# Hybrid decoder step: one dense group of the last mLSTM chunk placed behind the sums of the latent squares

## The reference

```python
def layer(x, ...):
    h = rmsnorm(x, lw['norm_mix'])
    z = h @ lw['w_in']
    qm, km, vm, om, im, fm, cq, ckv, kr = jnp.split(z, splits, axis=-1)
    hm, C, n, m = mlstm_chunkwise(qm, km, vm, ig, lf, C0, n0, m0)
    hm = rmsnorm(hm, lw['m_norm']) * jax.nn.sigmoid(om)
    lat = concatenate([rmsnorm(ckv, lw['mla_kv_norm']), rope(kr, pos)])
    qa = rmsnorm(cq, lw['mla_q_norm']) @ lw['mla_w_uq']
    ...   # latent attention, output projection, ConvFFN, embedding gate
```

## Time and profile before

| | us |
|---|---|
| median of three runs | 3328.66 |
| lowest, highest | 3320.07, 3329.58 |
| profiled execution | 3329.29 |
| its span | 3327.5 |
| mean granted clock, share of full | 0.958 |

### The profile page before, as it was taken

The page is one execution under the profiler, slowest core; times in us unless marked ns, Lnnn a source line. Parts: engine busy times, 40 slices in busy tenths (PEclk is TensorE's granted clock), DMA queues, the critical chain, the costliest instruction groups (busy, mean ns, idle before and its releaser), DMA issues. The chain is left out here.

```text
span 3327.5 us, 49163 instructions
## 1 busy us (share of the span) xinstructions
PE 3087.8 (93%) x19219; PEld 2874.2 (86%) x19219; DVE 1524.3 (46%) x2458; ACT 1067.3 (32%) x1982; POOL 144.3 (4%) x260
## 2 busy tenths in 40 slices
PE   4999999889999999988989999989899999999887
PEld 4998755789999999988989986559899999999886
DVE  4223643345454554447351345434554544454653
ACT  4323332324333323334242342322432323233341
POOL 0000300000000000000000012000000000000000
PEclk9999999889999999998989988989899999999988
DMA  5101252211111111102131023421111111111023
GB/s 212 52 26 44 86 172 70 103 56 51 39 39 52 46 44 51 39 18 90 40 123 41 16 99 101 133 60 81 68 40 50 51 39 51 39 39 51 6 103 131
DMA packets 60916, 220.53 MB, mean 66 GB/s; under 512 B 6922, under 2 KB 26890, under 8 KB 45842
## 3 DMA queue, kind: packets, MB, share of 16 engines
q1 hardware_dynamic: 60690, 217.27, 18.5%
HBM read 189.72 MB, written 27.52 MB: 65 GB/s over the span
## 5 line engine op out<-in xcount | busy, mean ns | idle before, releaser
L210 PE MATMUL psum<-h_high,conv_ffn_weight_parts 128*128 128x352 f32 x2112 | 690.4, 327 | 21.9 <-DVE h_low L315 14.3
L212 PE MATMUL psum<-h_high,conv_ffn_weight_parts 128*128 128x352 f32 x2112 | 686.7, 325 | 0.0
L211 PE MATMUL psum<-h_low,conv_ffn_weight_parts 128*128 128x352 f32 x2112 | 682.6, 323 | 0.0
L1990 DVE SCALAR_TENSOR_TENSOR conv_sum<-u_padded,vectors,conv_sum 128x1024 f32<-128x1024 f32 x176 | 226.1, 1285 | 595.1 <-ACT conv_sum L1939 582.6
L210 PEld LDWEIGHTS psum<-h_high,conv_ffn_weight_parts 128*128 128x128 f32 x2112 | 400.8, 190 | 24.9 <-issue 22.0
L211 PEld LDWEIGHTS psum<-h_low,conv_ffn_weight_parts 128*128 128x128 f32 x2112 | 399.3, 189 | 0.0
L212 PEld LDWEIGHTS psum<-h_high,conv_ffn_weight_parts 128*128 128x128 f32 x2112 | 397.1, 188 | 0.0
L210 PE MATMUL psum<-g_parts,conv_ffn_weight_parts 128*128 128x352 f32 x1056 | 345.3, 327 | 27.1 <-DVE g_parts L2001 16.3
L212 PE MATMUL psum<-g_parts,conv_ffn_weight_parts 128*128 128x352 f32 x1056 | 343.1, 325 | 0.0
L211 PE MATMUL psum<-g_parts,conv_ffn_weight_parts 128*128 128x352 f32 x1056 | 342.8, 325 | 0.0
L2009 DVE TENSOR_TENSOR x<-x,psum 128x352 f32<-128x352 f32 x528 | 255.5, 517 | 118.3 <-PE psum L212 117.9
(11 more groups left out here) (330 smaller groups left out, 5389.5 us busy)
## 6 DMA issues: line engine op xcount, KB each, us to landing
conv_ffn_weight_stage<-w_up_dram SPq DMA_DIRECT2D x44, 1024.0 KB, 4.8
conv_ffn_weight_stage<-w_down_dram SPq DMA_DIRECT2D x22, 1024.0 KB, 4.8
_projection_weight_stage<-w_in_dram SPq DMA_DIRECT2D x18, 1024.0 KB, 4.8
pages<-cache_dram SPq DMA_DIRECT2D x64, 288.0 KB, 4.2
pages<-cache_dram SPq DMA_DIRECT2D x64, 160.0 KB, 2.5
mix_work<-x_residual SPq DMA_DIRECT2D x16, 528.0 KB, 3.8
x<-x_residual SPq DMA_DIRECT2D x2, 4224.0 KB, 17.0
x_residual<-x SPq DMA_DIRECT2D x16, 528.0 KB, 2.7
```

The source lines that it names most:

```text
L210: pe.matmul(out, lhs[0], rhs[0], start=first, stop=False)
L211: pe.matmul(out, lhs[0], rhs[1], start=False, stop=False)
L212: return pe.matmul(out, lhs[1], rhs[0], start=False, stop=last)
L1990: dve.scalar_tensor_tensor(t[:, q, 0:SEQ], row[:, tap:tap + SEQ], w, t[:, q, 0:SEQ], ALU.mult, ALU.add).then_inc(ph["conv_step"], 1)
```

## The change

In the last chunk (c = 7) TensorE starts with `spread(7)` and no dense group in front of it. The first two dense groups then stand where the second and the third stood, and the third is issued after the sums of the latent squares; after it come the wait for the last evacuation and the transposes. The sums go to banks `B_S` and `B_S + 1` (5 and 6) instead of 0 and 1. ScalarE in the last chunk does `decays(7)` before it evacuates the first group, and after the second evacuation takes the square roots, `squares(7)`, and the last evacuation. VectorE takes the reciprocal between the outputs and the state updates of chunk 7 instead of at its end. SyncE's program is as it was.

```diff
--- before.py
+++ after.py
@@ -669,6 +669,9 @@
                     dve.tensor_tensor(vTM[:, c, i::2, 0:M_DV], num[:, i, :, 0:M_DV],
                                       den[:, 1, i::2].unsqueeze(2).to_broadcast([P, 2, M_DV]),
                                       ALU.mult).then_inc(ph["h_made"], 1)
+                if c == NCK - 1:
+                    dve.wait_ge(ph["rt_step"], 2)
+                    dve.reciprocal(mem.rt[:, 1], mem.rt[:, 0]).then_inc(ph["rs_made"], 1)
                 dve.wait_ge(ph["qa_made"], 3 * (c + 1))
                 for h in range(M_HEADS):
                     s = state[part(h), h // 2, :]
@@ -712,8 +715,6 @@
                 outputs(c)
                 if c in (1, 3):
                     ring.lo(dve, 7 + c // 2, JW)
-            dve.wait_ge(ph["rt_step"], 2)
-            dve.reciprocal(mem.rt[:, 1], mem.rt[:, 0]).then_inc(ph["rs_made"], 1)
 
         @block.scalar
         def _(act):
@@ -818,18 +819,23 @@
             act.wait_ge(ph["state_zeroed"], 2)
             act.wait_ge(ph["cwc_made"], 2)
             for c in range(NCK):
-                evacuate(MIXED + 3 * c)
+                if c < NCK - 1:
+                    evacuate(MIXED + 3 * c)
                 decays(c)
                 if 4 <= c < 7:
                     latent_squares(c)
+                if c == NCK - 1:
+                    evacuate(MIXED + 3 * c)
                 evacuate(MIXED + 3 * c + 1)
-                evacuate(MIXED + 3 * c + 2)
-                if c == NCK - 1:
-                    for i, d in enumerate((Q_RANK, KV_RANK)):
-                        act.wait_ge(ph["lsum_done"], i + 1)
-                        act.activation(mem.rt[:, 0, i, :], ps[:, i, 0:TT], ACT.Sqrt, bias=core.eps,
-                                       scale=1.0 / d).then_inc(ph["rt_step"], 1)
-                squares(c)
+                if c < NCK - 1:
+                    evacuate(MIXED + 3 * c + 2)
+                    squares(c)
+            for i, d in enumerate((Q_RANK, KV_RANK)):
+                act.wait_ge(ph["lsum_done"], i + 1)
+                act.activation(mem.rt[:, 0, i, :], ps[:, B_S + i, 0:TT], ACT.Sqrt, bias=core.eps,
+                               scale=1.0 / d).then_inc(ph["rt_step"], 1)
+            squares(NCK - 1)
+            evacuate(len(GROUPS) - 1)
 
         @block.tensor
         def _(pe):
@@ -919,20 +925,29 @@
             pe.wait_ge(ph["ones_made"], 1)
             pe.wait_ge(ph["state_zeroed"], 3)
             pe.wait_ge(ph["cwc_made"], 2)
-            for c in range(NCK):
+            def latent_sums(i, squares):
+                for c in range(TT):
+                    mm = pe.matmul(ps[:, B_S + i, c:c + 1], squares[:, token_tile(c)], core.ones[:, 0:1],
+                                   start=(c == 0), stop=True, skip_group_check=True)
+                mm.then_inc(ph["lsum_done"], 1)
+
+            for c in range(NCK - 1):
                 dense(MIXED + 3 * c)
                 spread(c)
                 dense(MIXED + 3 * c + 1)
                 scores(c)
                 dense(MIXED + 3 * c + 2)
                 values(c)
+            spread(NCK - 1)
+            dense(len(GROUPS) - 3)
+            scores(NCK - 1)
+            dense(len(GROUPS) - 2)
+            values(NCK - 1)
+            pe.wait_ge(ph["lsq_added"], 3)
+            latent_sums(0, core.norm)
+            latent_sums(1, mem.sqk)
+            dense(len(GROUPS) - 1)
             pe.wait_ge(ph["bank_free"], len(GROUPS))
-            pe.wait_ge(ph["lsq_added"], 3)
-            for i, squares in enumerate((core.norm, mem.sqk)):
-                for c in range(TT):
-                    mm = pe.matmul(ps[:, i, c:c + 1], squares[:, token_tile(c)], core.ones[:, 0:1],
-                                   start=(c == 0), stop=True, skip_group_check=True)
-                mm.then_inc(ph["lsum_done"], 1)
             pe.wait_ge(ph["rs_made"], 1)
             for c in range(TT):
                 tr = pe.transpose(ps[:, c // 4, c % 4 * P:(c % 4 + 1) * P],
```

## The result

| | before | changed |
|---|---|---|
| median, us | 3325.55 (6 runs, 3320.07 to 3329.58) | 3336.82 (6 runs, 3331.30 to 3339.20) |
| ratio | | 1.0033, 95% interval 1.0019 to 1.0047 |
| span of the profiled run, us | 3327.5 | 3330.0 |

The change costs 11.3 us by the medians, between 6 and 16 by the interval. The forecast stood on the median of the three runs taken first, 3328.66; all six runs of before have 3325.55, and against that median the forecast of +11.6 us reads 3337.2, where 3336.8 was measured. Of the 3.5 us between the recorded 3340.3 and the measured time, 3.1 are this shift of the base.

What follows compares the result with a forecast made beforehand. The prediction took whichever engine is last at the `mix_projection` barrier to set the price, with TensorE busy 93% of the span. Its terms summed to +5.8 us per layer, +11.6 over two, giving 3340.3 us from 3328.66; range 3331 to 3349.

Steps and rivals of the forecast that it cites:

- stall in front of `spread(7)`: Chunk 7: without a dense group as cover, TensorE idles until chunk 6's outputs are made; +1.0 us per layer.
- clock at `spread` and the group behind: Chunk 7: after the idle time the clock falls late in `spread`, slowing the dense group behind; +2.0 us per layer.
- latent sums: After `values(7)`: the sums still lose the clock but take 5.7 us; -0.6 us per layer, from -2.3 to +0.7.
- held-back group at low clock: Behind the sums: the third dense group begins at the low clock they left; +1.7 us per layer, 0 to +3.2.
- evacuation, transposes, stores: Phase end: the state store, delayed by the last evacuation, lands last at the barrier; +1.7 us per layer, +1.4 to +2.3.
- Rival A: Chunk 7: the clock is not lost at `spread(7)`, only in the sums; 3.8 us per layer, 3336.3 us, chance 0.18.
- Rival B: Last chunk: the clock is kept altogether because dense work follows at once; +0.4 us per layer, 3329.5 us, chance 0.08.
- Rival C: Phase end: the state store is hidden, tail 0 to 0.1 us; 4.1 us per layer, 3336.9 us, chance 0.1.
- Rival D: Phase end: held-back group wholly at half clock and store late; 7.9 us per layer, 3344.5 us, chance 0.12.
- Rival E: Last chunk: the group is not held back in effect because another wait binds; 3328.7 us, chance 0.02.

Runs made afterwards that it cites:

- wide sums: The changed kernel with each matmul of the latent sums streaming 128 columns of ones instead of one; 1.0016 of the kernel before.
- state store first: The changed kernel with the mLSTM state store put ahead of the last out-gate store in SyncE's order; 1.0032 of the kernel before.
- early half: The changed kernel with the third dense group moved back in front of the sums and the end ordered as before; 1.0024 of the kernel before.
- its two variants with wide sums: The kernel before with 128-column latent sums alone, 0.9996 of before; and with the sums of squares opening seven phases widened too, 0.9975.
- all three cures: The changed kernel with four useless matmuls filling the idle time before `spread(7)`, 128-column latent sums and the state store issued earlier; 0.9994 of before.

## Why the prediction was right, point by point

The sum was forecast at +5.8 us per layer. Over two profiles of each kernel, four layers, it was +4.3, and the timings gave 9.3 and 11.3 us for both layers, so the total of the timings is nearer to the forecast than two of its terms are. The mechanism was right: each loss is in the trace where the prediction put it. That +11.3 us came out beside +11.6 is partly luck. The traces hold 8.6, and two terms were each wrong by 1.2 us per layer.

| per layer, us | forecast | measured in the trace |
|---|---|---|
| stall in front of `spread(7)` | +1.0 | +1.0 (0.93 idle) |
| clock at `spread` and the group behind | +2.0 | +2.7 (8.97, 7.43, 8.97, 8.98 for 5.85) |
| latent sums | -0.6 | -1.8 (mean 4.5 for 6.3) |
| held-back group at low clock | +1.7 | +1.8 (mean 5.9 for 4.05 with its gap) |
| evacuation, transposes, stores | +1.7 | +0.5 (4.4 to 4.6 for 4.0) |

*The stall* came as computed, and nothing else in chunk 7 waits. *The clock at spread* was taken from the distance to the nearest row, and it falls in every one of the ten layers with the hole left open (the changed kernel twice, wide sums, state store first, early half); filling the hole removes the fall in all four layers of two kernels. Rival A is out. The moment varies: in two of the ten layers it fell in the hole itself, in others not before the dense group. *The held-back group* was sized by the dense work of the next phase that starts low, and that held: 1.4 to 2.6 us, 1.8 in the mean. Rival B, that the clock survives if dense work follows the sums at once, is out as well: the clock fell in all four layers before the group began. The rule of the Trainium skill on idle gaps ("TensorE: Matmul & The Clock Gate", section "HAM oscillation — how this bites in real kernels"), which stood beside rival B, did not decide here; the clock fell in stretches in which TensorE was 100% busy with one-column matmuls, and stayed when the same matmuls streamed 128 columns.

*The sums* were mis-sized. The forecast saw that a clock given back late would favour them, and took 0.6 us for it out of a range that reached to 2.3; it was 1.8. In the six layers of changed order whose clock had fallen at `spread` and come back (the changed kernel twice, state store first) it fell again 2.9 to 4.0 us into the sums; in the kernel before, in four layers, at 1.1 to 2.4. That fits the direction which the forecast gave. It is not shown as the cause: with the hole filled, and no earlier fall, it came at 4.0 and 1.7 us.

*The end* was mis-sized in its main term, the landing of the state store. It was read as 3.3 us from the earlier trace rows and was 2.0 to 2.2. Those rows hold a collision. The queues from 325 to 329 of the kernel before show a packet of instructions beside the store:

```profile
q1 hardware_dynamic: 144, 0.13, 10.2%
q8 instruction: 1, 0.02, 2.5%
...
state_p_out_dram<-mix_work SPq DMA_DIRECT2D x1, 129.0 KB, 3.6
```

and from 332.5 to 335.2 of the changed kernel none:

```profile
q1 hardware_dynamic: 288, 0.31, 32.6%
...
out_gate<-og_staging SPq DMA_DIRECT2D x1, 176.0 KB, 1.8
state_p_out_dram<-mix_work SPq DMA_DIRECT2D x1, 129.0 KB, 2.0
```

The other profiles bear this out. Ten stores had such a packet beside them in their first 2 us (the kernel before twice, its two variants with wide sums, and state store first) and landed in 2.5 to 3.8 us. Fourteen had none and landed in 2.0 to 2.4, most of them with the 176 KB out-gate store beside them. No run moved the packet by itself, so that it is the cause stays an argument from these rows.

The place of the store, last at the barrier, was right. Rival C was half right: the store landed sooner, as that rival said, but not soon enough to be hidden. Its condition did not come true, yet its sum, +4.1 us per layer, is nearer to the +4.3 of the traces than the forecast's +5.8.

Rival D is out in its second half, the late store; one of four held-back groups came near to its first half, at +2.6 us. Rival E is out: the group is held back and nothing else binds.

The two misses have one sign. Together they are 2.4 us per layer, less 0.7 that the clock at `spread` cost above its forecast and small change. That the medians of the first comparison still stood 11.3 us apart, not 8.6, is within their interval.

## What to carry to other kernels

A dense group is more than its own time: it covers waits, and in these runs TensorE kept its clock where one stood. Before one is taken out of a stretch of small matmuls, look for what it covered on VectorE and for what then stands side by side; a hole of 0.93 us cost 3.7 here. And where a matmul with one moving column is bound by the loading of its weights (PEld is busy all through the sums), give it as many columns as the pace allows: at the full clock 128 cost nothing here, and they can keep the clock for what follows.

## What the runs showed of the hardware

- fp32 matmuls of 128 columns go at the pace of those with one: 36 in 4.04 us, against 36 in 4.13 us for thin ones in layer 0 of the changed kernel, nearly all at the full clock. At the low clock 18 wide ones took 4.18 us, 18 thin ones 3.97.
- With thin latent sums the clock was lost in them, or in `values` just ahead, in all 16 layers of eight profiles. With wide ones it was kept through the sums and all that stood behind them up to the barrier in all eight layers of four.
- The nine transposes take 1.20 us at the full clock and 2.18 at the low one.
- The two layers of one execution, and two executions of one kernel, differ by up to 3 us in a stage whose clock falls, and by less than 0.05 us where it does not (25.61 us in all four layers of the two kernels before with wide sums, 27.20 in both with all three cures).
- The store of 129 KB landed in 2.0 to 3.8 us, with nothing changed in it: 2.5 to 3.8 with a packet of instructions beside it, 2.0 to 2.4 without.
